# A decoder step on one core: products before mixes in the merging loop, ten cache-shift pieces moved from the projection to the merging stage, and the semaphore clears moved beside the routing

## The chip, the core and the metric

The kernel runs on one core of one Trainium2 chip. A core has five engines that run their own instruction streams: TensorE (PE, matrix products, with a weight-load part shown as PEld), VectorE (DVE), ScalarE (ACT), GpSimd (POOL) and SyncE (SP), which here only issues transfers. Sixteen DMA engines carry the transfers; SP, ACT and POOL each feed a queue of their own (q1, q10 and q0 in the profile). The metric is device time in microseconds: a median of 1463.35 us over 3 runs (1461.33 to 1466.58) before the change.

## The reference

One inference step of a one-layer decoder for 512 prompt tokens and 8 sample tokens that share all weights (520 tokens, width 1024, float32):

```
h = rmsnorm(x)
[qA kA vA | qB kB vB | gate_a gate_b] = h @ w_in
branch A: stick-breaking attention, 8 heads x 64 (samples read 32 pages of 128 cached keys/values each)
branch B: dilated sliding-window softmax attention, 3 groups x 4 heads x 64,
          windows 128, 512, 2048 (samples read caches cache_kv_b0/1/2)
x = x + (sigmoid(gate_a) * (oA @ w_br_a) + sigmoid(gate_b) * (oB @ w_br_b)) @ w_o
x = x + hier_moe(rmsnorm(x))     top-1 of 4 groups, top-2 of 8 experts in it, 32 SwiGLU experts
y = rmsnorm(x)
```

It also returns the new keys and values, and the three sample caches of branch B moved on by one row (`new_kv_b*_sample`: every old row but the first, then the new one). That move is a plain copy from device memory to device memory, about 42 MB.

## The kernel before, in words

The program is a row of stages, each of them a block in which every engine has its own hand-written stream; between two blocks all engines meet at a barrier. Nothing is scheduled by a tool: the order is the order of the code.

- `prepare`: norm and transposes of x.
- `project` (30 to 399 us): 46 column tiles of `w_in`. Tile t is 16 products of 128x260 (L508), each in two passes; the weights come in pairs of tiles, 1 MB per load, into two buffers (`w_slots`, L194), so the load for pair m is issued when pair m-2 has been used (`sp.wait_ge(s["made"], 2 * m - 2)`). ACT copies each tile out of PSUM (L531). Meanwhile POOL gathers 64 groups of cached keys, 1 MB each, into a ring of five buffers, and DVE multiplies and sums each (L569, L576). At the end DVE and ACT turn the scores into log weights (L595 to L613) with help of two products of PE (L494, L495).
- `attend` (399 to 674 us): branch A and B for the prompt, values of branch A for the samples.
- `merge` (674 to 861 us): in a loop over eight column tiles PE computes `tile(t)`: 8 products with `w_br_a` (L1092) and 2 with `w_br_b` (L1100, both in two passes), and DVE `mix(t)`: three operations that multiply by the gates and add (L1267, L1273, L1277). Interleaved runs branch B for the samples: PE's `replicate(b)` spreads a sample's query over all partitions (L1082) and DVE's `scores(b)` multiplies it with the cached keys and sums (L1287, L1291). PE's `replicate(b)` waits for `rep_used`, which DVE gives when the multiplications of `scores(b-1)` are done. Then ten half blocks with `w_o` (L1110), norms, transposes and router logits; ACT loads the cached values of branch B (24 loads, L281) once the scores are final, and PE's `values` (L1158) waits for them. SP writes the normalised rows (`h_rows`, L1073).
- `route` (861 to 896 us): top-k and slot tables. SP starts the first expert weights (ten loads of 1 MB).
- `clear_semaphores`: a block of its own in which POOL clears the 117 semaphores of all stages before, one instruction each (L170).
- `experts` (906 to 1434 us): 32 experts, 6 MB of weights each, in a ring of 12 buffers.
- `finish`.

The copy of the caches is cut into 45 pieces (`shift_pieces()`), mostly of 1 MB in runs of 8 KB: 16 runs for each of 8 samples. All are issued by SP. `IN_PROJECT` counts those issued in `project`: `early` ones before its loop, and one behind each of the loads m = 2, 3, ... of `w_in`. `attend` issues 16, and `merge` the rest, behind its own loads.

```
pieces = shift_pieces()[:IN_PROJECT]
early = IN_PROJECT - (N // 2 - 2 - 4)
...
if 2 <= m < 2 + len(pieces) - early:
    shift(k, sp, pieces[early + m - 2:early + m - 1])
```

Of the kernel before, what the change touches and what calls it, by code (L numbers as in the profile page):

```python
# [141 lines left out]
class Kernel:  # L142
# [17 lines left out]

        return self.ctx.enter_context(self.nc.semaphore(name))

    def clear_semaphores(self):

        with self.nc.Block() as block:  # L165

            @block.gpsimd
            def _(pool):
                for sem in self.sems:
                    pool.sem_clear(sem)  # L170
        self.sems = []

    def const(self, name, rows=P):
        a, b = self.at[name]
# [61 lines left out]


SHIFT_PIECE = 16 * SHIFT_RUN
IN_PROJECT = 22
IN_ATTEND = 2 * DEC  # L240


# [134 lines left out]
def project(k):  # L377
# [11 lines left out]
    N = TILES + GATE_TILES  # L389
# [4 lines left out]
    with ExitStack() as ctx:  # L394
# [32 lines left out]
        with nc.Block() as block:  # L427

            @block.sync
            def _(sp):  # L430
                pieces = shift_pieces()[:IN_PROJECT]
                early = IN_PROJECT - (N // 2 - 2 - 4)
                shift(k, sp, pieces[:early])
                for m in range(2, N // 2):
                    sp.wait_ge(s["made"], 2 * m - 2)
                    load_w_in(k, sp, m)
                    if 2 <= m < 2 + len(pieces) - early:
                        shift(k, sp, pieces[early + m - 2:early + m - 1])
                    if m == 6:
                        sp.wait_ge(s["laid"], 8)  # L440
                        sp.dma_start(io["o_ka"].rearrange("(b p) n -> p b n", p=P), krows[:, :, 0:WA])\
                            .then_inc(k_out, 16)
                    if m == 8:
                        sp.wait_ge(s["laid"], 12)
                        sp.dma_start(io["o_va"].rearrange("(b p) n -> p b n", p=P), k.v_rows[:, :, 0:WA])\
                            .then_inc(v_out, 16)
                    if m == 14:
                        sp.wait_ge(s["laid"], 24)
                        for g in range(NG):
                            keep = min(GROUPS[g][0], SEQ) // P  # L450
                            sp.dma_start(io[f"o_kvp{g}"][:, 0:WBO].rearrange("(b p) n -> p b n", p=P),
                                         krows[:, NB - keep:NB, g * WBO:(g + 1) * WBO]).then_inc(k_out, 16)
                    if m == 17:
                        sp.wait_ge(s["laid"], 30)
                        for g in range(NG):
                            keep = min(GROUPS[g][0], SEQ) // P
                            sp.dma_start(io[f"o_kvp{g}"][:, WBO:2 * WBO].rearrange("(b p) n -> p b n", p=P),
                                         k.v_rows[:, NB - keep:NB, WA + g * WBO:WA + (g + 1) * WBO])\
                                .then_inc(v_out, 16)
                        sp.dma_start(io["o_kas"], k.samp[0:DEC, WA:2 * WA]).then_inc(k_out, 16)  # L460
                        sp.dma_start(io["o_vas"], k.samp[0:DEC, 2 * WA:3 * WA]).then_inc(v_out, 16)
                        for g, (wlen, _) in enumerate(GROUPS):
                            for c, sem in ((0, k_out), (1, v_out)):
                                at = 3 * WA + (1 + c) * WB + g * WBO
                                sp.dma_start(io[f"o_kvs{g}"][:, wlen - 1, c * WBO:(c + 1) * WBO],
                                             k.samp[0:DEC, at:at + WBO]).then_inc(sem, 16)
                sp.wait_ge(k_out, 16 * (2 + 2 * NG))
                sp.wait_ge(v_out, 16 * (2 + 2 * NG))
# [148 lines left out]
def attend(k):  # L617
# [39 lines left out]
    with ExitStack() as ctx:  # L657
# [31 lines left out]
        def used_all(eng, b):  # L689

            n = N_GROUPS + b * GROUPS_K + GROUPS_K - 1
            eng.wait_ge(k.ring_used[n % RING], n // RING + 1)

        with nc.Block() as block:

            @block.sync
            def _(sp):
                sp.dma_start(k.tables_b[:], k.io["consts"][:, k.at["rel"][0]:k.at["row_bias"][0]])\
                    .then_inc(tables_in, 16)
                for b in range(DEC):  # L700
                    if b:
                        used_all(sp, b - 1)
                    shift(k, sp, shift_pieces()[IN_PROJECT + 2 * b:IN_PROJECT + 2 * b + 2])
                    if b == 5:
# [295 lines left out]
def merge(k):  # L1000
# [15 lines left out]
    with ExitStack() as ctx:  # L1016
# [36 lines left out]
        with nc.Block() as block:  # L1053

            @block.sync
            def _(sp):
# [11 lines left out]
                    .then_inc(s["route_in"], 16)  # L1068
                shift(k, sp, shift_pieces()[IN_PROJECT + IN_ATTEND:])
                for b in range(NBLK):  # L1070
# [188 lines left out]
            def _(dve):  # L1259
# [59 lines left out]
                                           k.const("ident", DEC)[:, 0:DEC].unsqueeze(2).to_broadcast(  # L1319
                                               [DEC, DEC, SLOTS_B]), ALU.mult))  # L1320
                for t in range(KC):
                    mix(t)
                    if t >= 2:
                        scores(t - 2)
                for a, e in ((0, EARLY_TILES), (EARLY_TILES, KC)):
                    link(dve.tensor_copy(gate_s[:, a:e], gate_of(k, a, e)[:, :, 1, SEQ:TOK]))
                scores(6)
# [55 lines left out]
def route(k):  # L1383
# [4 lines left out]
    NR = E_GROUPS + EXPERTS  # L1388
    MUL = TOK // SLOT
    BIG = 64.0  # L1390
    with ExitStack() as ctx:
        small = lambda name, *shape: k.sb("rt_" + name, [P, NBLK, *shape], ctx=ctx)
        lg = k.lg
# [33 lines left out]
        with nc.Block() as block:  # L1427

            @block.sync
            def _(sp):  # L1430
                for n, slot in enumerate((0, 1, 2, 3, 6, 7, 8, 9)):
                    load_half(k, sp, slot, (0, 2, 1, 3)[n % 4], n // 4)
                for n in range(2):
                    load_half(k, sp, 10 + n, 4 + n, 0)

            @block.scalar
            def _(act):
# [120 lines left out]
def load_half(k, sp, slot, q, e):  # L1558

    name, c = (("w_gate_e", KC), ("w_up_e", KC), ("w_down_e", FC))[q // 2]  # L1560
    rows = slice(q % 2 * c // 2, (q % 2 + 1) * c // 2)
    sp.dma_start(k.raw[:, slot].rearrange("p (c n) -> p c n", c=c // 2),
                 k.io[name][0, bass.ds(e, 1)].rearrange("a (p c) n -> p (a c) n", c=c)[:, rows])\
        .then_inc(k.raw_in[slot // 2], 16)
# [339 lines left out]
def build(nc, io, at, stop=99):  # L1904
    with ExitStack() as ctx:
        k = Kernel(nc, ctx, io, at)
        k.consts = k.sb("consts_sb", [P, at["rel"][0]])
        k.g_attn = k.sb("g_attn_sb", [P, KC])
        k.b_sb = k.sb("b_sb_sb", [P, HA])
        k.run = k.sb("run_sb", [P, N_GROUPS], U32)  # L1910
        k.shifted = ctx.enter_context(nc.semaphore("shifted"))
        steps = STEPS[:stop]
        k.oT = k.sb("oT", [P, (WA + WBO) // P, TOK])
        k.samp = k.sb("samp", [P, TILES * P])
        k.h2_out = ctx.enter_context(nc.semaphore("h2_out"))
        k.v_rows = k.sb("v_rows", [P, NB, WA + WB])
        k.x1 = k.v_rows[:].rearrange("p b n -> p (b n)").rearrange("p (b n) -> p b n", n=D)
        k.lg = k.sb("lg", [P, NBLK, E_GROUPS + EXPERTS])
        k.gate = k.sb("gate", [P, NBLK, 2])
        k.index = k.sb("index", [SLOT, 2, ALL_SLOTS + 2], U32)  # L1920
        k.owner = k.sb("owner", [1, MORE], I32)
        k.n_more = k.sb("n_more", [1, 1], I32)
        with ExitStack() as inner:
            k.qk = k.sb("qk", [P, QK_TILES, TOK], ctx=inner)
            k.scores = k.sb("scores", [P, DEC, HA, PAGES], ctx=inner)
            k.ring = k.sb("ring", [P, RING, ROWS_K * WA], ctx=inner)
            k.ring_in = [k.sem(f"ring_in{n}", inner) for n in range(RING)]
            k.ring_used = [k.sem(f"ring_used{n}", inner) for n in range(RING)]
            k.keys_in = [k.sem(f"keys_in{n}", inner) for n in range(2)]
            k.gates_in = [k.sem(f"gates_in{n}", inner) for n in range(2)]  # L1930
            k.wa_in, k.wb_in = k.sem("wa_in", inner), k.sem("wb_in", inner)
            with ExitStack() as projecting:
                k.hT = k.sb("hT", [P, KC, TOK], ctx=projecting)
                k.w = k.sb("w_slots", [P, 2, KC, 2 * P], ctx=projecting)
                k.w_in = [k.sem(f"w_in{j}", projecting) for j in range(2)]
                for f in steps[:2]:
                    f(k)
            with ExitStack() as attending:
                k.tables_b = k.sb("tables_b", [P, at["row_bias"][0] - at["rel"][0]], ctx=attending)
                for f in steps[2:3]:  # L1940
                    f(k)
            for f in steps[3:4]:
                f(k)
        k.raw = k.sb("raw", [P, RING_W, HALF])
        k.raw_in = [ctx.enter_context(nc.semaphore(f"raw_in{q}")) for q in range(RING_W // 2)]
        for f in steps[4:5]:
            f(k)
        k.clear_semaphores()
        for f in steps[5:]:
            f(k)  # L1950
        if stop > 3:
            with nc.Block() as block:
                @block.sync
                def _(sp):
                    sp.wait_ge(k.shifted, 16 * len(shift_pieces()))
# [28 lines left out]
```

## Time and profile before

| what | value |
|---|---|
| median of 3 runs | 1463.35 us |
| profiled execution | 1465.87 us, span 1464.1 us |
| PE busy | 1199.8 us (82%) |
| DVE busy | 584.0 us (40%) |
| ACT busy | 250.3 us (17%) |
| POOL busy | 278.4 us (19%) |
| DMA | 455.45 MB, mean 311 GB/s |
| mean granted TensorE clock | 0.914 |

Times within the span are microseconds from its start. A row of the timeline gives start, duration, engine, line, operation, what it writes and reads, the count of merged instructions, and in brackets how long the engine sat idle just before and what ended that. PEclk is the granted share of the full TensorE clock, 1.00 being 2.4 GHz and 0.50 being 1.2 GHz. DMA share is the mean busy share of the 16 DMA engines. "PEq L427" and the like as the end of a wait is a barrier between blocks.

### The profile page before, as it was taken

The page shows a single profiled execution, that of the slowest core. Times are in us where ns is not written, and L with a number is a line of the kernel's source. Part 1 is how long each engine was busy: PE and PEld are TensorE (multiplying, and loading weights), DVE is VectorE, ACT ScalarE, POOL GpSimd, SP SyncE. Part 2 cuts the span into 40 slices and gives each one's busy share as a digit, 9 for nine tenths or more (in the row PEclk, how much of TensorE's full clock was granted, in tenths as well). Part 3 has the DMA queues.
Part 4 walks back from the last instruction along what each step waited for, and adds up shares of the span by engine and source line. Part 5 has one row for each costly group of instructions (what it writes and reads, how often), then busy time and mean ns, then how long its engine had stood idle before and what let it go on. Part 6 is the DMA issues. An engine that isn't in the chain of part 4 may idle for free. (4 is left out here: it accounts for less than half of the span.)

```text
span 1464.1 us, 14582 instructions
## 1 busy us (share of the span) xinstructions
PE 1199.8 (82%) x5502; PEld 690.0 (47%) x5502; DVE 584.0 (40%) x762; ACT 250.3 (17%) x401; POOL 278.4 (19%) x205
## 2 busy tenths in 40 slices
PE   4999999979969998989789961987887888778870
PEld 3878888868734444446444541333332332223320
DVE  2099999998444344432333133111111111111115
ACT  2121111100343334420002110110101010101012
POOL 1045455553012222220000000111111111111110
PEclk9999999989979999997779975999999899999995
DMA  5889999998249798997803042899999999999954
GB/s 187 325 298 383 379 382 380 397 408 332 85 146 357 316 366 340 358 381 275 277 0 115 28 186 111 337 403 411 410 408 400 410 407 409 400 408 406 412 221 189
DMA packets 104324, 455.45 MB, mean 311 GB/s; under 512 B 13613, under 2 KB 45661, under 8 KB 57445
## 3 DMA queue, kind: packets, MB, share of 16 engines
q1 hardware_dynamic: 72469, 301.43, 52.6%
q0 software_dynamic: 24176, 144.13, 25.4%
q10 hardware_dynamic: 7632, 9.25, 1.8%
q8 instruction: 31, 0.51, 0.1%
q14 instruction: 16, 0.13, 0.0%
HBM read 442.10 MB, written 65.44 MB: 347 GB/s over the span
## 5 line engine op out<-in xcount | busy, mean ns | idle before, releaser
L508 PE MATMUL proj_ps<-hT,w_slots 128*128 128x260 f32 x1472 | 332.9, 387 | 15.2 <-DMA w_slots<-in_w_in 12.8
L508 PEld LDWEIGHTS proj_ps<-hT,w_slots 128*128 128x128 f32 x1472 | 280.0, 192 | 66.4 <-DMA w_slots<-in_w_in 13.9
L1782 PE MATMUL ex_gp<-raw,ex_xT 128*64 128x512 f32 x1024 | 232.9, 602 | 22.6 <-DMA raw<-in_w_up_e 14.8
L1796 PE MATMUL ex_yp<-raw,ex_hmT 128*64 128x512 f32 x512 | 138.0, 688 | 68.6 <-DMA raw<-in_w_down_e 68.1
L209 POOL DMA_INDIRECT ring<-in_cache_k_a,run_sb x64 | 139.7, 2183 | 192.6 <-DVE scores L576 164.2
L569 DVE TENSOR_TENSOR ring<-ring,q_rep 128x2048 f32<-128x2048 f32 x64 | 145.9, 2281 | 41.6 <-ACT q_rep L553 41.1
L1782 PEld LDWEIGHTS ex_gp<-raw,ex_xT 128*64 128x64 f32 x1024 | 70.6, 138 | 161.1 <-issue 123.9
L576 DVE TENSOR_REDUCE scores<-ring 128x32 f32<-128x2048 f32 x64 | 145.8, 2280 | 0.0
L1737 DVE TENSOR_TENSOR ex_hm<-ex_sg,ex_gp 64x512 f32<-64x512 f32 x32 | 21.7, 679 | 269.7 <-ACT ex_sg L1717 269.7
L1796 PEld LDWEIGHTS ex_yp<-raw,ex_hmT 128*64 128x64 f32 x512 | 42.4, 155 | 162.6 <-issue 115.3
L209 POOL DMA_INDIRECT ring<-in_cache_v_a,run_sb x64 | 73.4, 1146 | 238.3 <-PE at_vp L761 222.2
L1689 POOL DMA_INDIRECT pair_rows<-ex_yg,ex_to x32 | 29.5, 922 | 431.6 <-PE ex_xp L1770 428.0
L1743 DVE COPY ex_yg<-ex_yp 64x512 f32<-64x512 f32 x32 | 21.8, 682 | 161.1 <-PE ex_yp L1796 161.1
L761 PE MATMUL at_vp<-ring,at_w 128*32 128x512 f32 x512 | 69.7, 621 | 4.1 <-DMA ring<-in_cache_v_a,run_sb 4.1
L1110 PE MATMUL mg_ps<-mg_wo,mg_mix 128*128 128x512 f32 (+1 forms) x160 | 72.2, 607 | 0.0
L1717 ACT ACTIVATE ex_sg<-ex_gp 64x512 f32<-64x512 f32 x32 | 19.0, 593 | 253.0 <-PE ex_gp L1782 253.0
L1770 PEld LDWEIGHTS ex_xp<-consts_sb,ex_xg 64*128 64x128 f32 x264 | 31.6, 201 | 43.1 <-issue 43.1
L1722 ACT ACTIVATE ex_yg<-ex_yp 64x512 f32<-64x512 f32 x32 | 19.0, 594 | 188.1 <-PE ex_yp L1796 188.1
L1670 POOL DMA_DIRECT2D ex_opened<-in_g_final x2 | 1.1, 568 | 258.1 <-POOLq L165 258.1
L1770 PE MATMUL ex_xp<-consts_sb,ex_xg 64*128 64x64 f32 x264 | 36.1, 278 | 16.6 <-DMA ex_xg<-h_rows,ex_from 16.6
L778 PE MATMUL at_sp<-qk 64*128 64x256 f32 (+3 forms) x96 | 37.5, 471 | 13.4 <-DVE at_sc L888 13.4
L737 PE MATMUL at_zp<-at_soft,consts_sb 128*128 128x128 f32 (+3 forms) x160 | 38.8, 400 | 8.9 <-DVE at_soft L863 8.9
(249 smaller groups left out, 1080.7 us busy)
## 6 DMA issues: line engine op xcount, KB each, us to landing
raw<-in_w_gate_e SPq DMA_DIRECT2D x64, 1024.0 KB, 22.7
raw<-in_w_up_e SPq DMA_DIRECT2D x64, 1024.0 KB, 27.6
raw<-in_w_down_e SPq DMA_DIRECT2D x64, 1024.0 KB
o_kvs<-in_cache_kv_b SPq DMA_DIRECT2D x39, 1024.0 KB
w_slots<-in_w_in SPq DMA_DIRECT2D x23, 1024.0 KB, 12.1
qk<-in_cache_kv_b ACTq DMA_DIRECT2D x36, 128.0 KB, 2.9
gate_rows<-stage ACTq DMA_DIRECT2D x16, 260.0 KB, 6.3
mg_wo<-in_w_o SPq DMA_DIRECT2D x1, 4096.0 KB, 24.4
```

Source lines behind the costliest of these rows:

```text
L209: pool.indirect_dma_start(k.ring[:, n % RING, :], None, runs, bass.IndirectOffsetOnAxis(ap=k.run[:, i:i + 1], axis=0), bounds_check=runs.s ...
L508: last = pe.matmul(pp[:, j, half, 0:H], w[:, m % 2, c, j * P:(j + 1) * P], k.hT[:, c, half * H:(half + 1) * H], start=(c == 0), stop=(c == ...
L569: dve.tensor_tensor(v, v, qrep[:, n // GROUPS_K, :].unsqueeze(1).to_broadcast([P, ROWS_K, WA]), ALU.mult).then_inc(multiplied, 1)
L576: dve.tensor_reduce(k.scores[:, b, :, at:at + ROWS_K].rearrange("p h r -> p r h")[:, ::-1], k.ring[:, n % RING, :].rearrange("p (r h d) -> ...
L737: last = pe.matmul(zp[:, at:at + n], k.const("later_eq" if kb2 == kb else "ones"), soft[:, OFF[kb2]:OFF[kb2] + n], start=(kb2 == kb), stop ...
L761: last = pe.matmul(vp[r * PAD:(r + 1) * PAD, :], wt[:, h % 2, column(g, r), :], k.ring[:, n % RING, r * WA:(r + 1) * WA], start=(g == 0), ...
L778: pe.matmul(sps[:, 0:w], b_rows(slot, g, Q_TILE)[:, qb * P:(qb + 1) * P], b_rows(slot, g, K_TILE)[:, lo * P:lo * P + w], start=True, stop= ...
L1110: last = pe.matmul(ps[0:r, n % 2, :], mixT[:, c, b * P:b * P + r], wo[:, c, h * 512:(h + 1) * 512], start=(c == 0), stop=(c == KC - 1))
L1689: pool.indirect_dma_start(k.io["pairs"], bass.IndirectOffsetOnAxis(ap=to_row[:, j, :], axis=0), yg[:, j, :], None, bounds_check=2 * TOK - ...
L1770: last = pe.transpose(xp[:, c, :], v[:, c, :], k.const("ident", SLOT)[:, 0:SLOT])
L1782: last = pe.matmul(gp[at:at + SLOT, j], xT[:, c, :], raw[:, slot, c1 * FF:(c1 + 1) * FF], start=(c == 0), stop=(c == KC - 1))
L1796: last = pe.matmul(yp[h * SLOT:(h + 1) * SLOT, j], hmT[:, c, :], raw[:, slot, o:o + 512], start=(c == 0), stop=(c == FC - 1))
```

## The change

Three things. `IN_PROJECT` goes from 22 to 12 with `early` held at 5, so that the loads m = 9 to 18 of `w_in` no longer have a piece behind them; `attend` still issues 16 pieces (other ones, of the same size), and `merge` issues 17 where it issued 7. In the merging loop of DVE `scores(t - 2)` stands ahead of `mix(t)`. And the semaphores of the stages before `route` are cleared by POOL within the block of `route`; the block that did only this is gone (the six semaphores of `route` itself are not cleared).

```
-    def clear_semaphores(self):
-
-        with self.nc.Block() as block:
-
-            @block.gpsimd
-            def _(pool):
-                for sem in self.sems:
-                    pool.sem_clear(sem)
-        self.sems = []
+    def done_semaphores(self):
+
+        done, self.sems = self.sems, []
+        return done
...
-IN_PROJECT = 22
+IN_PROJECT = 12
...
-                early = IN_PROJECT - (N // 2 - 2 - 4)
+                early = 5
...
                 for t in range(KC):
-                    mix(t)
                     if t >= 2:
                         scores(t - 2)
+                    mix(t)
...
+    done = k.done_semaphores()
...
+            @block.gpsimd
+            def _(pool):
+                for sem in done:
+                    pool.sem_clear(sem)
...
-        k.clear_semaphores()
```

Lines below the first edit have other numbers in the changed kernel (five less in `project` and `merge`: L1082 of before is a product of PE in both, but DVE's L1287 is L1282 there).

The first place is DVE in the merging loop, tiles 2 and 3. `mg_mix` and the `samp<-ring` row are the mixes, `samp<-qk` and `mg_sc` the products and sums of the samples' scores. Before:

```order
L1267 TENSOR_TENSOR mg_mix<-ring,mg_ps 128x520
L1273 TENSOR_TENSOR samp<-ring,mg_ps 128x512
L1277 TENSOR_TENSOR mg_mix<-mg_mix,samp 128x512
L1287 TENSOR_TENSOR samp<-qk,mg_ps 128x256
L1287 TENSOR_TENSOR samp<-qk,mg_ps 128x128 x2
L1287 TENSOR_TENSOR samp<-qk,mg_ps 128x256
L1291 TENSOR_REDUCE mg_sc<-samp 128x3x4
L1267 TENSOR_TENSOR mg_mix<-ring,mg_ps 128x520
```

The same place after the change:

```order
L1282 TENSOR_TENSOR samp<-qk,mg_ps 128x256
L1282 TENSOR_TENSOR samp<-qk,mg_ps 128x128 x2
L1282 TENSOR_TENSOR samp<-qk,mg_ps 128x256
L1286 TENSOR_REDUCE mg_sc<-samp 128x3x4
L1262 TENSOR_TENSOR mg_mix<-ring,mg_ps 128x520
L1268 TENSOR_TENSOR samp<-ring,mg_ps 128x512
L1272 TENSOR_TENSOR mg_mix<-mg_mix,samp 128x512
L1282 TENSOR_TENSOR samp<-qk,mg_ps 128x256
```

The products of sample t-2, which need only PE's `replicate(t - 2)`, now come ahead of the mixes of tile t, which need PE's `tile(t)`.

The second place is SP in the projection, from the load m = 17 of `w_in` (`w_slots`) to the last. `o_kvs<-in_cache_kv_b` is a shift piece, `o_kvp`, `o_kas`, `o_vas` and `o_kvs<-samp` are the new keys and values on their way out. Before:

```order
L194 DMA w_slots<-in_w_in 128x8x256
L233 DMA o_kvs<-in_cache_kv_b 16x8x2048
L457 DMA o_kvp<-v_rows 128x256
L457 DMA o_kvp<-v_rows 128x4x256 x2
L460 DMA o_kas<-samp 8x512
L461 DMA o_vas<-samp 8x512
L465 DMA o_kvs<-samp 8x256 x6
L194 DMA w_slots<-in_w_in 128x8x256
L233 DMA o_kvs<-in_cache_kv_b 16x8x2048
L194 DMA w_slots<-in_w_in 128x8x256 x4
```

After (the first row holds the loads m = 15 to 17):

```order
L189 DMA w_slots<-in_w_in 128x8x256 x3
L452 DMA o_kvp<-v_rows 128x256
L452 DMA o_kvp<-v_rows 128x4x256 x2
L455 DMA o_kas<-samp 8x512
L456 DMA o_vas<-samp 8x512
L460 DMA o_kvs<-samp 8x256 x6
L189 DMA w_slots<-in_w_in 128x8x256 x5
```

The two pieces of this stretch are gone, the writes stay between the loads m = 17 and 18.

The third place is SP in the merging stage, behind its loads, after the change; before, the first row was x5:

```order
L228 DMA o_kvs<-in_cache_kv_b 16x8x2048 x15
L228 DMA o_kvs<-in_cache_kv_b 15x8x2048
L228 DMA o_kvs<-in_cache_kv_b 8x1536
L1068 DMA h_rows<-ring 128x1024 x4
L1068 DMA h_rows<-samp 8x1024
```

The ten pieces stand behind all of merging's loads on SP and ahead of the `h_rows` writes.

## Rows read from the trace of the kernel before

**Rows 1.** Busy time by stage: window, us, busy us per engine, clock, DMA share, GB/s.
```profile
30.00:400.00 370.00, 353.21 (x1604) 295.55 (x1605) 301.82 (x149) 57.61 (x111) 148.59 (x69) 0.99 0.88 336
...
906.00:1434.00 528.00, 419.80 (x1928) 160.07 (x1928) 62.82 (x163) 58.96 (x98) 61.97 (x68) 0.94 0.94 378
```

**Rows 2.** Timeline, PE in the projection: the waits for a load of weights.
```profile
268.26 7.28 PE L508 MATMUL proj_ps<-hT,w_slots 128*128 128x260 f32 x32 [2.20 <-DMA w_slots<-in_w_in]
...
321.18 65.14 PE L508 MATMUL proj_ps<-hT,w_slots 128*128 128x260 f32 x288 [10.02 <-DMA w_slots<-in_w_in]
```

**Rows 3.** Timeline, ACT in the projection: the copies of tiles 35 and 36.
```profile
311.19 0.60 ACT L531 ACTIVATE stage<-proj_ps 128x520 f32<-128x520 f32 x1 [6.41 <-PE proj_ps L508]
...
330.24 0.60 ACT L531 ACTIVATE stage<-proj_ps 128x520 f32<-128x520 f32 x1 [18.44 <-PE proj_ps L508]
```

**Rows 4.** SP's issues of loads m = 17 and 18 of w_in; load 18's landing.
```profile
283.14 0.57 SPq L194 DMA_DIRECT2D w_slots<-in_w_in  x1
...
299.17 2.21 SPq L194 DMA_DIRECT2D w_slots<-in_w_in  x1
...
DMA to landing us min/median/max: 22.0/22.0/22.0
```

**Rows 5.** Timeline, DVE, ACT and PE at the projection's end.
```profile
355.68 1.23 DVE L595 TENSOR_SCALAR q_rep<-scores 128x2048 f32<-128x2048 f32 x1
...
366.30 1.28 ACT L556 ACT_TABLE_LOAD   x1 [0.39 <-ACT stage L531]
...
380.32 1.23 DVE L609 TENSOR_TENSOR_SCAN oT<-oT 128x512 f32<-128x512 f32 x1
...
386.15 1.96 PE L494 MATMUL rep_ps<-q_rep,consts_sb 128*128 128x512 f32 x2
```

**Rows 6.** Timeline, merging loop: tile 2, the start of tile 3, the first half block.
```profile
687.51 1.55 PE L1082 MATMUL mg_ps<-samp,consts_sb 8*128 8x384 f32 x4
...
688.99 3.77 PE L1092 MATMUL mg_ps<-oT,qk 128*128 128x260 f32 x16
...
692.60 1.88 PE L1100 MATMUL mg_ps<-oT,scores 128*128 128x512 f32 x4
...
695.92 1.14 DVE L1287 TENSOR_TENSOR samp<-qk,mg_ps 128x256 f32<-128x256 f32 x4
...
697.12 2.92 PE L1082 MATMUL mg_ps<-samp,consts_sb 8*128 8x384 f32 x4 [2.63 <-DVE samp L1287]
...
699.97 5.56 PE L1092 MATMUL mg_ps<-oT,qk 128*128 128x260 f32 x16
...
761.43 8.83 PE L1110 MATMUL mg_ps<-mg_wo,mg_mix 128*128 128x512 f32 x16
```

**Rows 7.** Waits of the whole span: that of replicate for the products.
```profile
PE mg_ps L1082 <- DVE samp L1287: 15.8, 6, 2.6
```

**Rows 8.** Busy time in two windows of the merging stage.
```profile
710.00:730.00 20.00, 17.37 (x46) 11.26 (x47) 5.07 (x10) 0.00 (x0) 0.00 (x0) 0.74 0.95 286
730.00:774.00 44.00, 36.10 (x82) 18.96 (x81) 17.40 (x38) 0.00 (x0) 0.00 (x0) 0.81 0.00 0
```

**Rows 9.** Timeline, merging: a held issue on SP, the values' loads on ACT, their reader.
```profile
675.63 8.56 SPq L1059 DMA_DIRECT2D v_rows<-in_x_prompt  x1
...
774.37 11.45 ACTq L281 DMA_DIRECT2D qk<-in_cache_kv_b  x24
...
785.87 1.06 ACT L1227 ACTIVATE ring<-v_rows 128x1024 f32<-128x1024 f32 x1 [112.04 <-issue]
...
786.20 7.13 PE L1110 MATMUL mg_ps<-mg_wo,mg_mix 128*128 128x512 f32 x16
...
803.48 1.48 PE L1158 MATMUL mg_ps<-samp,mg_pn 8*32 8x256 f32 x6
```

**Rows 10.** Timeline, DVE: the first instruction of the routing, and of the experts.
```profile
860.86 0.17 DVE L1472 TENSOR_REDUCE rt_mx<-lg 128x5 f32<-128x20 f32 x1 [0.55 <-PEq L1053]
...
905.84 1.76 DVE L1753 MEMSET ex_xg<- 64x2048 f32 x1 [9.93 <-PEq L165]
```

## The prediction

> **What bounds the kernel now.** I read the busy time by stage first, then the waits of the whole span, then the timeline around each place that the change touches. In the projection [rows 1] PE is busy 353 of 370 us and the DMA share is 0.88; in the experts' stage the DMA share is 0.94 over 528 us, so that stage is a stream of weights that starts when its block starts and moves as a whole. The stages stand one behind another with barriers between, so what a stage loses or gains on its own last-ending engine reaches the end in full. The question at each of the three edits is which engine ends the stage there.
>
> **Projection.** PE stands still for a load of weights twice late in the stage, 2.20 us and 10.02 us [rows 2]. The second costs more than it shows: ACT's copies of two neighbouring tiles are 330.24 - 311.19 = 19.05 us apart where 6.41 + 0.60 = 7.01 us is the rule [rows 3], so 12.04 us went, some 2 of them to a slower tile after the wait. Together 14.2 us. The load that PE waits for, m = 18, was issued at 299.17 and took 22.0 us to land [rows 4]. From the issue of load 17 at 283.14 to that landing at 321.2 SP's queue carried, in 38 us, load 17, a shift piece, the new values (about 1.15 MB) and load 18: some 4.2 MB. Without the piece 3.2 MB are left; at the same rate that is 29 us, a landing at 312, against 309 at which PE would be there (311.2 less the 2.2 of the first wait). So an estimated 3 us of waiting would stay. The pieces of the pairs before are gone too and leave the queue shorter at 283, which makes it less; I take a remainder of 2. Gain 12; ends 2 (the writes alone hold load 18 up) and 14.
>
> Is anything late next? The DVE works on cached keys until shortly before its clamp and gains nothing from PE being sooner. It ends the clamp at 355.68 + 1.23 = 356.9, and ACT takes it up only at 366.30, so 9.4 us lie between; behind ACT's part the DVE has its totals ready at 380.32 + 1.23 = 381.6, and PE comes for them at 386.15: another 4.6 [rows 5]. PE may come 9.4 + 4.6 = 14.0 us sooner before it waits for them. The gain of 12 passes, one of 14 just so.
>
> **Merging loop.** Six times PE waits for the DVE's products before it can spread the next sample's query, 15.8 us in all [rows 7]. In tile 2 there is no such wait: from the start of `replicate` at 687.51 to the end of the last product, 692.60 + 1.88 = 694.48, it is 6.97 us. Then PE stands for 2.63 us while the DVE mixes tile 2 and multiplies for sample 0, and the next tile's 16 products take 5.56 us instead of 3.77 [rows 6]; in 710 to 730 us the granted clock is 0.74 [rows 8]. With the products of sample t-2 ahead of the mixes of tile t, the DVE does them while PE works on tile t (5.5 us), and the wait is gone for each of the six. The DVE's work in a tile fits into 7 us: products 1.14, three mixes of 0.72 each (two of them lie between 694.48 and 695.92) and a sum that I put at no more than its products, 4.5 in all. So six tiles of 6.97 us from 687.51, then the last mix behind the last product (two operations and their starts, 1.6 us), and the first half block starts at 687.51 + 41.8 + 1.6 = 730.9 where it started at 761.43: 30.5 us. That half block took 8.83 us against 7.13 of a later one [rows 6, 9], 1.7 more of gain if the clock is up. Together 32. Lower end: the waits go and the slow clock stays, 16 to 20. What it reads is there in time: merging's loads stand ahead of the pieces in SP's queue, and even the pieces were done by 730 [rows 8], when the first half block would ask for the last large one.
>
> A rule speaks against the clock's part. The Trainium skill (TensorE: Matmul & The Clock Gate, "A second HAM failure mode: psum-queue depth-cycling") tells of a kernel in which short idle gaps between groups of products, as it cycled through banks, were enough to make the clock swing; this loop cycles through eight banks. By it the sum's 32 would be 18. The row of tile 2, 3.77 us behind a gap with no wait in it, speaks for the full clock.
>
> **Clearing.** The DVE's first instruction of the experts comes 9.93 us after its last of the routing; the like step from merging to routing takes 0.55 [rows 10]. One barrier and the clears leave the path: 9.4 us. POOL has nothing else in the routing's 35 us, and clears that took less than 9.4 fit. Ends 8.5 and 9.4.
>
> **Ten pieces in merging.** In 710 to 730 the pieces moved at 286 GB/s with a share of 0.95, so a piece of 1.05 MB takes 3.5 us of all engines, and from 730 to 774 nothing moves at all [rows 8]. The pieces ended at about 729; ten more end at 764. Into that now come the values' loads: ACT issues them from 774.37 - 32 = 742.4 on, for 11.45 us, and PE asks for them at 803.48 - 32 = 771.5 [rows 9]. Left of the pieces at 742.4 are 21.6 us, and the values are about 11 us of work themselves (they can't take more than their issue if nothing else runs). Shared in halves they land at 765: no wait. If the pieces keep nearly everything, all is done at 775: a wait of 3.5. Then there is the issue itself. SP was held for 8.56 us on one load when much stood before it in its queue [rows 9]. If ACT is held likewise until the values are nearly in, its norm of block 0, at 785.87 - 32 = 753.9 in the new time, comes up to 21 us late. PE asks for the rows of that block at 786.20 + 7.13 = 793.3, 7.5 us behind the norm's start, and some part of these 7.5 is slack, so it would wait 14 to 21: I put it at 18. Ends 0 and 18; I take 3, near the end where the queue isn't full.
>
> The Trainium skill (DMA: Bandwidth & Descriptors, "Queues, rings and completion order") says that a DMA engine takes turns between queues by whole packets of some 9 to 17 descriptors. The values' runs are 1 KB and the pieces' 8 KB, so by it the values would get about a ninth of the bytes: the case of 3.5 us, and the sum would be half a microsecond less. No row before shows the two queues against each other with such runs.
>
> **Sum.** 12 + 32 + 9.4 - 3 = 50.4 us off 1465.87, the profiled execution (span 1464.1 and 1.8 around it): 1415.5. That execution lies 2.5 above the median of the runs, so for the median 1463.35 - 50.4 = 1413.
>
> **Rivals.**
> - The clock stays low in the loop. For it: every tile from the third on begins slow. Against: each of those stands behind a wait that goes. Loop 18 instead of 32: 1427.
> - The writes of new values hold load 18 as before, not the pieces: both waits stand behind such writes on SP (o_kvp behind m = 14 and m = 17), and other loads with a piece ahead of them aren't waited for. Gain 2 instead of 12: 1423. Against it is the sum of bytes above.
> - ACT is held at issuing the values: 15 more than taken, 1428.
> - Slower than before: the pieces run so slowly in merging that the last `h_rows` write, which stands behind them on the same queue and for which SP must wait before the block ends, sets the stage's end. Merging would end about 829; to eat the other 53 us it would have to end at 882, so 17 pieces from 709 on would take 173 us, 10.2 us each. That is the point from which it decides. They take 3.5 in the very place, with other loads beside them at first, so I give it little. Price at 11 us each: 1477.
> - The change does nothing measurable, as where some wait not seen before takes back all of it. Nothing in the rows would do that: 1463.
>
> **How the numbers follow.** Forecast as worked out 0.62, low clock 0.12, writes hold the load 0.11, ACT held 0.10, slower 0.03, no change 0.02. The likeliest one's own range is 1405 to 1421 (projection 9 to 14, loop 28 to 33, wait 0 to 6). The next three cases lie at 1423 to 1428, and two of them together at 1437; with 1404 to 1433 about two in ten are left out. This kernel can be told from itself at about 0.3% (4.4 us): faster 0.95, same 0.02, slower 0.03.
>
> **What would show it.** In the changed profile: PE's wait for weights in 300 to 325 at 3 us or less and the copies of tiles 35 and 36 at most 10 us apart; the stage's end near 387. In the loop no wait of `replicate` for the products, 7 us from tile to tile, clock 1.00 and the first half block 43 to 44 us behind the start of tile 2. The DVE's wait at the experts' start under 1 us. DMA busy for some 90 us from merging's start and PE's wait before `values` 0 to 4 us. I am wrong if the loop's tiles still take 9 us or more, if PE now waits long at the log-weight products (DVE's chain late), or if ACT's issue of the values takes 20 us or more.

## The result, and the profile after

The changed kernel takes 1438.61 us (median of 4 runs, 1437.57 to 1442.62) against 1463.6 (4 runs): a ratio of 0.983, 95% interval 0.981 to 0.986. It is faster by 25 us, well clear of the spread of the runs; the forecast was 50, and the range ended at 1433. The profiled execution took 1438.35 us, its span is 1436.5. Between the two profiled executions 27.6 us of span went. By stage, each taken from one fixed issue of SP to the next, in us (the first row is where the stage ends, the last runs to the end of the span):

| stretch | before | after | gain |
|---|---|---|---|
| start to end of the projection (first load of `attend`) | 399.19 | 389.71 | 9.5 |
| `attend` (to the load of `w_o`) | 275.88 | 274.30 | 1.6 |
| `merge` (to the first expert weights) | 185.75 | 179.98 | 5.8 |
| `route`, clears, first experts (to the first load of the ring's second round) | 59.02 | 49.01 | 10.0 |
| the rest | 544.26 | 543.50 | 0.8 |

Forecast were 12, 0, 29, 9.4 and 0. What is missing lies nearly all in merging, 23 us of it. The small differences need care: over the profiles of this case the projection with ten pieces moved ends between 387.1 and 393.2, and `attend`, which always runs the same code, takes 268.2 to 275.9.

The timeline of the merging loop after, with what answers to [rows 6]. The columns are those of before; the rows are tile 2's three groups, the next `replicate` and products, and the first half block:

```profile
676.50 1.55 PE L1077 MATMUL mg_ps<-samp,consts_sb 8*128 8x384 f32 x4
...
677.99 3.77 PE L1087 MATMUL mg_ps<-oT,qk 128*128 128x260 f32 x16
...
681.60 1.88 PE L1095 MATMUL mg_ps<-oT,scores 128*128 128x512 f32 x4
...
683.41 1.55 PE L1077 MATMUL mg_ps<-samp,consts_sb 8*128 8x384 f32 x4
...
684.89 3.77 PE L1087 MATMUL mg_ps<-oT,qk 128*128 128x260 f32 x16
...
719.66 7.11 PE L1105 MATMUL mg_ps<-mg_wo,mg_mix 128*128 128x512 f32 x16 [0.19 <-DVE mg_mix L1272]
```

The waits of [rows 7] are gone, a tile takes 6.90 us, the products stay at 3.77, and the granted clock is 1.00 from 690 us to the end of the loop. From tile 2 to the first half block it is 43.2 us against 73.9, and that half block takes 7.11 instead of 8.83: the loop gives 32.5 us.

Then the timeline of ACT, PE and DVE from the value loads on, which answers to [rows 9]:

```profile
730.88 32.31 ACTq L276 DMA_DIRECT2D qk<-in_cache_kv_b  x24
763.24 1.06 ACT L1222 ACTIVATE ring<-v_rows 128x1024 f32<-128x1024 f32 x1 [100.47 <-issue]
...
767.56 1.97 PE L1116 MATMUL mg_ps<-consts_sb,ring 128*128 128x128 f32 x8 [17.72 <-DVE ring L1300]
770.53 0.52 PE L1143 MATMUL mg_ps<-consts_sb,mg_pr 32*128 32x32 f32 x3 [1.00 <-DVE mg_xs L1346]
...
771.40 8.70 PE L1105 MATMUL mg_ps<-mg_wo,mg_mix 128*128 128x512 f32 x16
...
781.74 1.48 PE L1153 MATMUL mg_ps<-samp,mg_pn 8*32 8x256 f32 x6
```

ACT takes 32.31 us to issue the 24 loads, where it took 11.45. Its norm of block 0 stands behind them, the DVE's scaling behind the norm, and PE waits 17.72 us for the scaled rows. The values themselves are in when PE comes for them: no wait stands at L1153. The starts of the 24 issues show how ACT was held: the first ten go out about 0.7 us apart, then three of the next four take 4.8, 10.5 and 3.5 us, and the last ten go out within 5.6 us from 757 us on, as the pieces run out.

The two queues in that time, from a view of the DMA engines in 745 to 750 us (queue, packets, MB, share of 16 engines):

```profile
q1 hardware_dynamic: 180, 1.29, 88.4%
q10 hardware_dynamic: 178, 0.16, 12.8%
```

and in 760 to 764, when the pieces are through:

```profile
q1 hardware_dynamic: 5, 0.02, 1.4%
q10 hardware_dynamic: 1471, 1.34, 98.3%
```

In this window the two queues move packet for packet, 180 to 178, though a packet of the pieces holds 8 KB and one of the values 1 KB. So ACT's queue gets about a ninth of the bytes, 0.16 of 1.45 MB. The engine stands in its issue in the same time; that it does so because its queue is full is the reading that fits, and the next experiments test it.

The projection, PE's waits for a load of weights (answers to [rows 2]):

```profile
294.33 14.29 PE L503 MATMUL proj_ps<-hT,w_slots 128*128 128x260 f32 x64 [1.02 <-DMA w_slots<-in_w_in]
311.46 42.35 PE L503 MATMUL proj_ps<-hT,w_slots 128*128 128x260 f32 x192 [2.84 <-DMA w_slots<-in_w_in]
355.54 21.31 PE L503 MATMUL proj_ps<-hT,w_slots 128*128 128x260 f32 x96 [1.73 <-DMA w_slots<-in_w_in]
```

Load 18 still comes 2.84 us late (18.1 us to landing, after 22.0 in [rows 4]), and two small waits, 1.02 and 1.73 us, stand where none stood; the wait of 2.20 us at 268 is gone. And the DVE at the experts' start (answers to [rows 10]):

```profile
880.22 1.76 DVE L1754 MEMSET ex_xg<- 64x2048 f32 x1 [1.08 <-PEq L1423]
```

### The profile page after: what moved, and what is told of

It reads as the page before. It is cut to its first block and busy times, and to the rows that moved or that the text cites. A ratio compares the mean times of both kernels' runs of the same rounds, so it can differ in the third digit from the quotient of the medians.

```text
span 1436.5 us, 14566 instructions
## 1 busy us (share of the span) xinstructions
PE 1193.6 (83%) x5502; PEld 685.4 (48%) x5502; DVE 584.3 (41%) x762; ACT 250.3 (17%) x401; POOL 277.5 (19%) x205
## 5 line engine op out<-in xcount | busy, mean ns | idle before, releaser
L1797 PE MATMUL ex_yp<-raw,ex_hmT 128*64 128x512 f32 x512 | 147.0, 727 | 65.3 <-DMA raw<-in_w_down_e 64.8
L1105 PEld LDWEIGHTS mg_ps<-mg_wo,mg_mix 128*128 128x128 f32 (+1 forms) x160 | 27.9, 179 | 40.8 <-issue 40.6
## 6 DMA issues: line engine op xcount, KB each, us to landing
w_slots<-in_w_in SPq DMA_DIRECT2D x23, 1024.0 KB, 10.5
```

Source lines behind the costliest of these rows:

```text
L1105: last = pe.matmul(ps[0:r, n % 2, :], mixT[:, c, b * P:b * P + r], wo[:, c, h * 512:(h + 1) * 512], start=(c == 0), stop=(c == KC - 1))
L1797: last = pe.matmul(yp[h * SLOT:(h + 1) * SLOT, j], hmT[:, c, :], raw[:, slot, o:o + 512], start=(c == 0), stop=(c == FC - 1))
```

## The experiments

They ran in three groups, each on a chip of its own and each compared with the kernel before on that chip, which took 1461.6, 1461.4 and 1461.3 us (13, 19 and 11 runs). Between groups compare the ratios, not the times. "Merge" below is the time from the load of `w_o` to the first expert weights, as in the table, and is that of one profiled execution for each kernel.

**The ten pieces back in the projection.** Products first and the clears beside the routing stay.

```
-IN_PROJECT = 12
+IN_PROJECT = 22
```

> The changed kernel with the ten pieces back in the projection; products first and the clears beside the routing stay. Theory (ACT's issue of the 24 value loads is held while seventeen pieces drain, and PE stands 17.7 us for the norm of block 0): with seven pieces the SP queue is empty when ACT issues, the issue takes 11 to 13 us, PE's wait at the first transposes of the merging stage is under 1 us; the projection is as before. 1463.6 - 32 (loop) - 10 (clears) = 1421 to 1424. Rival (the faster loop itself leaves ACT and DVE late at the half blocks, whatever the pieces do): the wait of 17 us stays, 1446 to 1450.

1422.76 us, ratio 0.976 (0.972 to 0.980). ACT issues the loads in 11.44 us again, PE has no wait behind the first half block but the two at the end, merge is 151.9 us. The theory holds: with the pieces away the loop's gain is whole, and the changed kernel's merge of 180.0 us is 28.1 us longer for the ten pieces.

```profile
738.36 11.44 ACTq L276 DMA_DIRECT2D qk<-in_cache_kv_b  x24
749.85 1.06 ACT L1222 ACTIVATE ring<-v_rows 128x1024 f32<-128x1024 f32 x1 [78.19 <-issue]
```

**Only the ten pieces moved.**

```
-IN_PROJECT = 22
+IN_PROJECT = 12
...
-                early = IN_PROJECT - (N // 2 - 2 - 4)
+                early = 5
```

> The kernel before with the ten pieces moved and nothing else: mixes first, clears in a block of their own. Theory: the slow loop gives the pieces their time; they are through some 90 to 93 us from merging's start, ACT issues the value loads at 100, so they cost nothing or a few us there, and the projection gains 9.5: 1454 (1452 to 1457). Rival (ten more pieces in merging cost their 26 us wherever they run, through the DMA engines or the clock): 1475 to 1482. Second rival (the projection's gain is not of the pieces): 1463.

1452.59 us (10 runs), ratio 0.993 (0.991 to 0.996), as expected. The projection ends at 388.80, merge is 182.9 us, no more than before. The DMA share falls to 0.04 at 750 us and ACT issues the value loads only at 754.74, in 11.47 us: the slow loop ends after the pieces do, and 17 of them cost nothing there. The loss of the changed kernel belongs to neither part alone.

**Only the order of products and mixes.**

```
                 for t in range(KC):
-                    mix(t)
                     if t >= 2:
                         scores(t - 2)
+                    mix(t)
```

> The kernel before with products ahead of mixes and nothing else. Theory: the loop gains the whole 32 us (waits of replicate gone, clock 1.00) and nothing takes it back, since seven pieces end before ACT issues the value loads: 1431 to 1434. Rival (the faster loop itself makes the norm of block 0 late): only 5 to 8 us come out, 1456 to 1459.

1430.39 us, ratio 0.980 (0.977 to 0.983): 31 us, a little more than expected. Merge is 151.9 us against 185.8.

**Ten pieces behind the first `h_rows` write.** All of the change, but SP issues ten of merging's pieces once block 0 is scaled.

```
-                shift(k, sp, shift_pieces()[IN_PROJECT + IN_ATTEND:])
+                left = shift_pieces()[IN_PROJECT + IN_ATTEND:]
+                shift(k, sp, left[:7])
...
                     sp.dma_start(k.io["h2"][b * P:b * P + r, :], hn(b)[0:r, :]).then_inc(k.h2_out, 16)
+                    if b == 0:
+                        shift(k, sp, left[7:])
```

> The changed kernel with ten of merging's seventeen pieces behind the first h_rows write instead of ahead of it (SP issues them once block 0 is scaled, when the values are in). Theory: ACT is not held, PE's 17.7 us wait goes, the ten pieces run in a stretch where the DMA engines moved almost nothing, and all three gains come out: 1463.6 - 9.5 - 32 - 10 = 1412 (1410 to 1416). Rival (the pieces cost time wherever they run in merging): 1425 to 1438. Second rival (the last h_rows write behind the pieces ends the stage): 1416 to 1425.

1414.16 us, ratio 0.969 (0.966 to 0.972), as expected: faster than both kernels. The same ten pieces in the same stage, some 25 us later, cost 3.2 us (merge 155.1 against 151.9) instead of 28. The rows show the second group of pieces issued without hold, and DMA busy in what was the quiet stretch (second row: a window's busy time, with clock, DMA share and GB/s at its end):

```profile
744.19 7.13 SPq L228 DMA_DIRECT2D o_kvs<-in_cache_kv_b  x10
```

```profile
756.00:771.00 15.00, 15.00 (x92) 7.78 (x92) 0.68 (x3) 1.02 (x1) 0.00 (x0) 0.89 1.01 283
```

**Five pieces moved.**

```
-IN_PROJECT = 12
+IN_PROJECT = 17
```

> The changed kernel with five pieces moved instead of ten (those behind the loads m = 14 to 18): merging has twelve. Theory (ACT is held for as long as pieces are in flight once its own queue is full): in the changed kernel the pieces drained some 94 us from merging's start and ACT began to issue at 67; five pieces fewer at 3.5 us each end at 76, so ACT's issue is slow only at its start, the norm of block 0 comes 0 to 4 us late, and the projection keeps most of its gain, since the loads that PE waited for stand there: 1462 - 9 - 33 - 10 + 3 = 1413 (1410 to 1418). Rival (each piece in merging costs its share, 26 us for ten): 1423 to 1427.

1419.85 us, ratio 0.971 (0.968 to 0.974), between the two forecasts and nearer to mine. The projection ends at 388.42, so as far as these profiles tell (387.1 to 393.2 with ten moved) the five pieces behind loads 14 to 18 gave all of its gain and the other five nothing. ACT's issue takes 15.19 us, PE waits 0.60 and 1.81: 2.4 us, as expected. But merge is 162.5, 10.6 more than with the pieces back. Of this 1.3 us went before the half block at 742.23, where the loop's first products are slower, 2.8 from there to the half block at 753.51, where the two waits lie, and 6.6 behind it, where PE has no wait that the kernel with the pieces back hasn't. These 6.6 are slower products: the half block behind the short wait takes 8.80 us, some 30 us later comes a second slow stretch with the granted clock at 0.77 in 786 to 801 us, and the logits at 818.53 take 3.62 instead of 1.98. No wait stands right ahead of the second stretch:

```profile
753.51 8.80 PE L1105 MATMUL mg_ps<-mg_wo,mg_mix 128*128 128x512 f32 x16
...
785.05 4.47 PE L1174 MATMUL mg_ps<-oT,scores 128*128 128x8 f32 x32
789.38 1.95 PE L1116 MATMUL mg_ps<-consts_sb,ring 128*128 128x128 f32 x8
791.12 8.69 PE L1105 MATMUL mg_ps<-mg_wo,mg_mix 128*128 128x512 f32 x16
```

The same instructions with the pieces back:

```profile
788.57 3.63 PE L1174 MATMUL mg_ps<-oT,scores 128*128 128x8 f32 x32
792.06 1.12 PE L1116 MATMUL mg_ps<-consts_sb,ring 128*128 128x128 f32 x8
793.02 7.03 PE L1105 MATMUL mg_ps<-mg_wo,mg_mix 128*128 128x512 f32 x16
```

**The value loads issued by POOL.** The seventeen pieces stay.

```
-                act.wait_ge(s["scores"], 1)
-                load_samples_b(k, act, 1, range(DEC), s["values_in"])
...
+            @block.gpsimd
+            def _(pool):
+                pool.wait_ge(s["scores"], 1)
+                load_samples_b(k, pool, 1, range(DEC), s["values_in"])
```

> The changed kernel with the 24 value loads issued by POOL, which is idle there, instead of ACT; the seventeen pieces stay ahead of the h_rows writes. It tells the held engine from the late data. Theory (PE waited for the norm, since ACT stood in its issue): the norm of block 0 is on time and PE's 17.7 us wait at the first transposes goes; the data are as late as before, so a new wait of 3 to 10 us appears at the values (L1153): 1416 to 1424. Rival (the late data or the busy DMA engines are what costs): within 4 us of the changed kernel, 1435 to 1442.

1425.6 us, ratio 0.977 (0.973 to 0.981), just above my range. The norm is on time and the wait at the first transposes is gone, so that wait was the held engine's. But only 10 of the 28 us come back: merge is 170.0. The late data now show, 8.59 us at the values, and behind this wait PE is slow in two stretches (the values' second part takes 4.49 us instead of 2.80, the products at L1179 4.48 instead of 3.63). The pieces cost time in two ways, through the held engine and through the late data, and in the changed kernel the first hid the second:

```profile
728.00 12.86 POOL L276 DMA_DIRECT2D qk<-in_cache_kv_b  x24 [92.60 <-DVE mg_sc L1332]
732.92 1.06 ACT L1227 ACTIVATE ring<-v_rows 128x1024 f32<-128x1024 f32 x1 [73.50 <-DVE v_rows L1297]
...
765.50 2.73 PE L1158 MATMUL mg_ps<-samp,mg_pn 8*32 8x256 f32 x6 [8.59 <-DMA qk<-in_cache_kv_b]
```

**The norm of block 0 ahead of the value loads.**

```
                 act.wait_ge(s["scores"], 1)
+                norm(0)
                 load_samples_b(k, act, 1, range(DEC), s["values_in"])
-                norm(0)
```

> The changed kernel with ACT's norm of block 0 ahead of its 24 value loads instead of behind them; the seventeen pieces stay. Theory (ACT stands in its issue while pieces are in flight): the norm is on time and PE's first transposes don't wait, but ACT's next instruction behind the loads, the exponential of the samples' scores, comes when the loads are issued, some 94 to 100 us from merging's start, so PE waits 12 to 17 us at the next step, the turned probabilities (L1143): within 5 us of the changed kernel, 1434 to 1442. Rival (the norm of block 0 is the one late thing, and what follows has slack): 1418 to 1425.

1433.25 us, ratio 0.982 (0.977 to 0.986): just past my end of 1434 and far from the rival. By these runs it can't be told from the changed kernel, whose ratio is 0.983 (0.981 to 0.986). In the profile merge is 169.7, 10 us less. The wait changed its name, as it must if ACT is what is held:

```profile
739.52 24.46 ACTq L276 DMA_DIRECT2D qk<-in_cache_kv_b  x21
...
766.91 0.52 PE L1143 MATMUL mg_ps<-consts_sb,mg_pr 32*128 32x32 f32 x3 [15.75 <-DVE mg_xs L1346]
767.77 8.49 PE L1105 MATMUL mg_ps<-mg_wo,mg_mix 128*128 128x512 f32 x16
...
799.01 3.63 PE L1174 MATMUL mg_ps<-oT,scores 128*128 128x8 f32 x32
```

After the long wait one half block is slow, 8.49 us, and everything behind it runs as with the pieces back, L1174 too. So a long wait does not always bring the second slow stretch.

**The writes of the new values behind load 20.** The kernel before otherwise.

```
-                    if m == 17:
+                    if m == 20:
                         sp.wait_ge(s["laid"], 30)
```

> The kernel before with the writes of the new values and of the samples' rows (L457 to L465) behind the load m = 20 of w_in instead of m = 17; all 22 pieces stay in the projection. Theory (load 18 was late because writes and pieces both stood ahead of it): the wait of 10 us at 311 shrinks to 3 or less and the stage ends 7 to 10 us sooner, 1452 to 1456; a small wait may come at load 21. Rival (the pieces alone delay load 18): within 3 us of before, 1459 to 1463.

1457.81 us (10 runs, 1448.78 to 1465.76), ratio 0.997 (0.994 to 1.000). My expectation failed: the projection ends at 399.95, no sooner. The wait of 10 us was split, not taken away:

```profile
297.91 28.44 PE L508 MATMUL proj_ps<-hT,w_slots 128*128 128x260 f32 x128 [1.96 <-DMA w_slots<-in_w_in]
...
328.74 28.32 PE L508 MATMUL proj_ps<-hT,w_slots 128*128 128x260 f32 x128 [2.39 <-DMA w_slots<-in_w_in]
...
363.56 23.50 PE L508 MATMUL proj_ps<-hT,w_slots 128*128 128x260 f32 x96 [6.50 <-DMA w_slots<-in_w_in]
```

With all the pieces in the stage, moving the writes moves the wait. Fewer bytes in its last third take it away (with five pieces moved no wait for weights stands behind 283 us), another place for the same bytes doesn't.

**Only the clears beside the routing.** (Taken from the changed kernel, with the order and the pieces set back.)

> The kernel before with the clears beside the routing and nothing else. Theory: the DVE's wait at the experts' start goes from 9.9 us to under 1 and nothing else moves: 1451 to 1454. Rival (the weights' loads are not in sooner, so the experts' stage gives it back): 1458 to 1463.

1455.23 us (10 runs, 1443.83 to 1460.8), ratio 0.995 (0.992 to 0.998), just over my range. The first expert weights to the ring's next round are 49.6 us apart against 59.0, and with the loop's order alone they stay at 59.3: the clears give 9.5 in the stage. The median moved by 6, less than that; the runs spread over 17 us, and `attend` alone, with the same code, took 268.2 us in this profile against 275.9 before. The difference of 3 us is within this and stays unexplained.

**Five pieces moved, and these behind the first `h_rows` write** (the fourth kernel above with `IN_PROJECT = 17`).

> Five pieces moved instead of ten, and these five behind the first h_rows write: seven pieces ahead of the value loads, as in the kernel before. Theory: the projection keeps its gain (the five behind the loads m = 14 to 18 gave all of it), ACT is not held, and the five pieces run in the quiet stretch: 1410 to 1414, level with or 2 us under the version with ten late pieces. Rival (the ten late pieces there cost nothing, and five in the projection cost a wait): 1415 to 1419.

1416.05 us (6 runs, 1409.91 to 1418.28), ratio 0.968 (0.965 to 0.971): not to be told from the version with ten late pieces. Either is the one to keep. My range ended at 1414, and the time fell into the rival's, but not by the rival's cause: the projection ended at 385.51, sooner than in any other kernel here. The missing time is in merge, 158.5 us against 155.1, and it is products at a lower clock. ACT is not held (11.45 us), and PE has no wait in this stretch:

```profile
756.77 4.27 PE L1161 MATMUL mg_ps<-qk,mg_alone 128*32 128x256 f32 x48
...
777.94 4.69 PE L1177 MATMUL mg_ps<-oT,scores 128*128 128x8 f32 x32
```

```profile
755.00:760.00 5.00, 5.00 (x41) 2.24 (x44) 0.00 (x0) 0.00 (x0) 0.00 (x0) 0.66 0.87 270
780.00:785.00 5.00, 5.00 (x24) 4.57 (x24) 0.45 (x2) 0.53 (x1) 0.00 (x0) 0.53 0.00 0
```

The second of these windows has PE busy throughout, no transfers and a clock of 0.53. Both slow stretches are here with no wait ahead of either.

## Why the prediction was wrong

- **Merging loop, 32 us.** Right: 32.5 in the profile, 31 us alone. The clock came up with the waits. The Trainium skill (TensorE: Matmul & The Clock Gate, "A second HAM failure mode: psum-queue depth-cycling") tells of short idle gaps between groups of products that let the clock swing. The prediction priced this at 18, and it did not come: the granted clock is 1.00 in this loop. The trace doesn't test the page, though, since in the changed loop PE has none of these gaps: it is busy 20.00 of 20.00 us from 690 to 710, and its one wait up to the first half block is 0.19 us.
- **Clearing, 9.4 us.** Right in its stage: 9.93 us of wait became 1.08, the stage gave 10.0 in the changed kernel.
- **Projection, 12 us.** 9.5 came. The step "a remainder of 2" was too small: 1.02, 2.84 and 1.73 us remain. Load 18 landed at 311.4 instead of 312, as the sum of bytes had it, but the wait at 355 was not foreseen. The five profiled kernels with ten pieces moved gain 6 to 12 us here, so the size of this miss is itself uncertain.
- **Ten pieces in merging, 3 us.** This is the step that failed: "I take 3, near the end where the queue isn't full". It cost 26.7: 32.5 that the loop gave less 5.8 that the stage gained (28.1 against the kernel with the pieces back). The mechanism was named, with an end of 18, and PE's waits measured 17.72 and 1.00 of it. I took the near end with a chance of 0.10 for the far one, though the row of SP held for 8.56 us [rows 9] showed that an issue can be held when much stands before it. An estimate from the same rows would have come near: the pieces keep the engines until about 764 - 10 (in the changed kernel they ended near 757), and if 24 loads don't go into the queue before that, ACT is free only then. The Trainium skill (DMA: Bandwidth & Descriptors, "Queues, rings and completion order") says that each DMA engine takes turns between queues by packets. The trace agrees in the share of bytes, about a ninth for the values. I had let the page bear on the data's landing alone, not on the issue. The loads' order on ACT (the norm first: 15.75 us of wait at ACT's next result) and the engine (POOL: no wait for the norm) show that the wait of 17.72 is that of the issue.
- **The same step, the data.** It put the wait for late values at 3.5 us at most. With POOL issuing, where no engine was held, it was 8.59. In the changed kernel this is hidden behind the held ACT.
- **The rest of that step** is slower products: 26.7 less 18.7 is 8 us, for which I had no term, and so the far end of 18 was too low by 8. From the half block at 771.40 to the logits it is 6.5 us more than with the pieces back (71.0 against 64.5), with the granted clock at 0.78, 0.77 and 0.75 in three of five windows of some 15 us; with the pieces back it was 1.00, and 0.89 in the last. The slow half block right behind the long wait is common to the changed kernel and the norm first (8.70 and 8.49 us). The second slow stretch is not explained by the wait: it comes after 2.4 us of waits with five pieces moved and after none with five late pieces, and it stays away after 15.75 us with the norm first and with ten late pieces. What brings it stays open; each kernel has one profiled execution.

The forecast for all gains together, 1413, is near what the version with ten late pieces measures, 1414. Part of that is luck: there the projection gave 12.1 us, and the pieces cost 3.2 us with no engine held.

## What to carry to other kernels

An engine can be held in its own issues, as ACT and SP were here, and then all that stands behind them waits too: before a large background copy is put beside another engine's loads, ask what that engine has to compute behind its issues, and sum the bytes (and packets) in flight at that moment. When one part of a change speeds a stage up, the transfers of another part lose the time they were to hide in: the ten pieces were free beside the slow loop and cost 28 us beside the fast one. In this kernel the background copy belongs behind the last load that someone waits for, not behind the last load of SP's own list.

## What the runs showed of the hardware

- Two queues with work shared the DMA engines nearly packet by packet: 159 to 161, 180 to 178 and 179 to 218 packets in three windows of 5 us, with 8 KB against 1 KB in one.
- ACT issued ten loads of 128 KB some 0.7 us apart, and then three issues took 4.8, 10.5 and 3.5 us while the pieces were in flight; SP was held 27.6 us over seventeen pieces of 1 MB. POOL issued the same 24 loads beside the same pieces in 12.86 us and was not held.
- TensorE's clock fell while PE was busy throughout: 0.53 in 780 to 785 us of the kernel with five late pieces, with no wait ahead and no transfers. In four of the kernels (the changed one, five pieces moved, POOL issuing, five late pieces) this second slow stretch cost the same 3.3 us over the same three groups of products, in the others it didn't come.
- Executions of the kernel before ranged from 1452.8 to 1472.2 us over the 43 of the experiments, against 1461.3 to 1466.6 over the four of the result.
